# RmsNorm on one Trainium2 core: sums of squares accumulated in PSUM by eight 128x512 products, root and reciprocal on full tiles

## What is computed

```python
def rms_norm(x, g, eps=RMS_EPS):
    xf = x.astype(jnp.float32)
    y = xf * lax.rsqrt(jnp.mean(xf * xf, axis=-1, keepdims=True) + eps)
    return (y * g.astype(jnp.float32)).astype(x.dtype)
```

## Time and profile before

| | |
|---|---|
| three runs | 4704.64, 4706.24, 4707.51 us, median 4706.24 |
| span of the profiled execution, first to last instruction | 4705.5 us |
| mean granted clock of TensorE | 0.894 |
| TensorE, weight loads, VectorE, ScalarE busy | 86%, 68%, 44%, 29% of the span |
| line 501, 288 records | 60.1 us busy, 168.5 us idle before it, ended by line 520 |
| line 506, 144 records | 37.2 us busy, 21.2 us idle before it |
| line 520, 102 additions | 63.1 us busy |

### The profile page before, as it was taken

One profiled execution on the slowest core, in us unless ns is written; L12 is line 12 of the kernel. 1 busy time (PEld: TensorE's weight loads), 2 busy tenths in 40 slices (PEclk: granted clock), 3 DMA queues, 4 the chain that ended last, 5 costly groups with the idle time before them and its releaser, 6 DMA issues. The chain is left out here.

```text
span 4705.5 us, 54624 instructions
## 1 busy us (share of the span) xinstructions
PE 4033.5 (86%) x21065; PEld 3196.7 (68%) x21065; DVE 2084.3 (44%) x3286; ACT 1342.8 (29%) x1844; POOL 0.2 (0%) x4
## 2 busy tenths in 40 slices
PE   5899998988999798699978799782599957897998
PEld 4667886767788684588866688681477734676886
DVE  2374544134445424533243433426666644524333
ACT  2353433232343323232232332213211112223222
POOL 0000000000000000000000000000000000000000
PEclk9999998975899897799987899885699966998999
DMA  2201222210122220022210122210000000021221
GB/s 98 75 0 63 96 91 81 90 54 0 63 98 93 79 82 35 36 89 92 96 67 27 63 89 98 87 48 22 5 0 0 0 9 27 0 89 63 98 96 65
DMA packets 43350, 278.44 MB, mean 59 GB/s; under 512 B 5920, under 2 KB 6816, under 8 KB 10598
## 3 DMA queue, kind: packets, MB, share of 16 engines
q1 hardware_dynamic: 36576, 266.35, 16.0%
q10 hardware_dynamic: 6662, 10.53, 0.7%
HBM read 274.76 MB, written 2.11 MB: 59 GB/s over the span
## 5 line engine op out<-in xcount | busy, mean ns | idle before, releaser
L190 PE MATMUL PS<-XH,WH 128*128 128x512 f32 (+1 forms) x2848 | 1104.3, 388 | 75.0 <-DVEq L95 34.3
L191 PE MATMUL PS<-XL,WH 128*128 128x512 f32 (+1 forms) x2848 | 1106.4, 388 | 0.0
L192 PE MATMUL PS<-XH,WL 128*128 128x512 f32 (+1 forms) x2848 | 1100.2, 386 | 0.0
L146 DVE TENSOR_TENSOR WL<-W,WH 128x2048 fp32r<-128x2048 f32 x254 | 582.0, 2292 | 1007.2 <-ACT WH L136 1002.8
L136 ACT ACTIVATE WH<-W 128x2048 fp32r<-128x2048 f32 x254 | 485.4, 1912 | 1102.3 <-PE PS L260 686.5
L190 PEld LDWEIGHTS PS<-XH,WH 128*128 128x128 f32 x2848 | 540.7, 190 | 209.0 <-issue 61.2
L192 PEld LDWEIGHTS PS<-XH,WL 128*128 128x128 f32 x2848 | 541.8, 190 | 112.0
L191 PEld LDWEIGHTS PS<-XL,WH 128*128 128x128 f32 x2848 | 540.9, 190 | 111.7
L258 PE MATMUL PS<-HH,WH 128*128 128x512 f32 (+1 forms) x1024 | 402.0, 393 | 10.5 <-DVEq L95 9.3
L259 PE MATMUL PS<-HL,WH 128*128 128x512 f32 (+1 forms) x1024 | 400.3, 391 | 0.0
L260 PE MATMUL PS<-HH,WL 128*128 128x512 f32 (+1 forms) x1024 | 399.8, 390 | 0.0
(11 more groups left out here) (437 smaller groups left out, 5045.8 us busy)
## 6 DMA issues: line engine op xcount, KB each, us to landing
W<-in_weights SPq DMA_DIRECT2D x254, 1024.0 KB, 4.8
X<-in_x ACTq DMA_DIRECT2D x1, 2048.0 KB
out<-X ACTq DMA_DIRECT2D x1, 2048.0 KB, 7.1
consts<-in_consts ACTq DMA_DIRECT2D x1, 1025.0 KB
bias<-bias_spread ACTq DMA_DIRECT2D x4, 256.0 KB
w_gd<-in_w_gd ACTq DMA_DIRECT2D x1, 640.0 KB
rope<-in_c_rope ACTq DMA_DIRECT2D x1, 528.0 KB
ws<-in_ws ACTq DMA_DIRECT2D x1, 512.0 KB
```

Source lines behind the costliest of these rows:

```text
L146: P.e.tensor_tensor(K.WL[:, s, :], K.W[:, s, :], K.WH[:, s, :].bitcast(F32), ALU.subtract).then_inc(P.sem("weights_split"), P.adds("weight ...
L190: P.e.matmul(out, wh[:, k, c], xh[:, k, r], start=(k == 0), stop=False)
L191: P.e.matmul(out, wh[:, k, c], xl[:, k, r], start=False, stop=False)
L192: last = P.e.matmul(out, wl[:, k, c], xh[:, k, r], start=False, stop=(k == KT - 1))
```

## The change

`RmsNorm` no longer adds squares on VectorE and builds no diagonals. TensorE multiplies each of the eight tiles of squares, as moving operand, by the 128x128 matrix of 1/1024 and accumulates in one PSUM bank (two with 528 tokens), which gives the mean already spread over the partitions. ScalarE takes the root from PSUM with eps as bias, on 128x512, into `R`; VectorE takes the reciprocal of 128x512 in place, and scales the tiles by `R` in SBUF instead of a row in PSUM. A pair of columns with eps joins the constants. Two counts of `norm_mean` keep `CentreV`'s semaphore in step.

```diff
     def act(self, K, P):
...
         split_last(K, P, split_act)
-        P.e.wait_ge(P.sem("norm_inverse"), P.due("norm_inverse"))
-        for r in self.columns(K):
-            last = P.e.activation(r, r, ACT.Sqrt)
+        P.e.wait_ge(P.sem("norm_mean"), P.due("norm_mean"))
+        for part, (t0, tn) in enumerate(self.toks):
+            last = P.e.activation(K.R[:, t0:t0 + tn], K.PS[:, part, 0:tn], ACT.Sqrt, bias=K.eps_col[:, 0:1])
         last.then_inc(P.sem("norm_root"), P.adds("norm_root"))
...
     def pe(self, K, P):
 
-        P.e.wait_ge(P.sem("norm_summed"), P.due("norm_summed"))
-        for j, (part, c, n) in enumerate(self.blocks()):
-            t = self.toks[part][0] + c
-            for half in range(2):
-                last = P.e.matmul(K.PS[0:n, 0, 2 * j:2 * j + 2], K.Y[:, half, t:t + n], K.inv_d[:, 0:2], start=(half == 0), stop=(half == 1))
+        for k in range(KT):
+            P.e.wait_ge(P.sem("norm_squared"), P.due("norm_squared"))
+            for part, (t0, tn) in enumerate(self.toks):
+                last = P.e.matmul(K.PS[:, part, 0:tn], K.inv_d[:, :], K.Y[:, k, t0:t0 + tn], start=(k == 0), stop=(k == KT - 1))
         last.then_inc(P.sem("norm_mean"), P.adds("norm_mean"))
-
-        for j, (part, c, n) in enumerate(self.blocks()):
-            P.e.wait_ge(P.sem("norm_diagonal"), P.due("norm_diagonal"))
-            last = P.e.matmul(K.PS[:, 6 + part, c:c + n], K.ones_row[0:n, 0:128], K.R[0:n, 16 + 128 * (j % 4):16 + 128 * (j % 4) + n], start=True, stop=True)
-            last.then_inc(P.sem("norm_spread"), P.adds("norm_spread"))
...
     def dve(self, K, P):
 
-        for k in range(2, KT):
-            P.e.wait_ge(P.sem("norm_squared"), P.due("norm_squared", 3 if k == 2 else 1))
...
-            last = P.e.tensor_tensor(y, y, K.Y[:, k, self.t0:self.t1], ALU.add)
...
+        P.count("norm_mean", 1)
         split_last(K, P, split_dve)
...
+        P.e.wait_ge(P.sem("norm_root"), P.due("norm_root"))
+        P.e.reciprocal(K.R[:, self.t0:self.t1], K.R[:, self.t0:self.t1]).then_inc(P.sem("dve_order"), P.adds("dve_order"))
         P.e.wait_ge(P.sem("dve_order"), P.due("dve_order", 0))
...
-            P.e.tensor_scalar(K.R[0:n, at:at + n], K.ident[0:n, 0:n], K.R[0:n, j:j + 1], None, ALU.mult).then_inc(P.sem("norm_diagonal"), P.adds("norm_diagonal"))
...
+        r = K.R[:, self.t0:self.t1]
```

More of the change, by code:

```diff
@@ L468 @@
     after_sums = before_panels = False
-    def blocks(self):
-        out = [(part, c, min(128, tn - c)) for part, (t0, tn) in enumerate(self.toks) for c in range(0, tn, 128)]
-        return sorted(out, key=lambda b: -b[2])
-    def columns(self, K):
-        n, rows = len(self.blocks()), self.blocks()[-1][2]
-        return [K.R[:, 0:4]] + ([K.R[0:rows, 4:n]] if n > 4 else [])
     def act(self, K, P):
@@ L513, in dve @@
     def dve(self, K, P):
-        for k in range(2, KT):
-            P.e.wait_ge(P.sem("norm_squared"), P.due("norm_squared", 3 if k == 2 else 1))
-            if k >= 4:
-                P.e.wait_ge(P.sem("norm_partial"), P.due("norm_partial", 0, less=1))
-            y = K.Y[:, k % 2, self.t0:self.t1]
-            last = P.e.tensor_tensor(y, y, K.Y[:, k, self.t0:self.t1], ALU.add)
-            last.then_inc(P.sem("norm_summed" if k == KT - 1 else "norm_partial"), P.adds("norm_summed" if k == KT - 1 else "norm_partial"))
-        split_last(K, P, split_dve)
-        blocks = self.blocks()
-        P.e.wait_ge(P.sem("norm_mean"), P.due("norm_mean"))
-        for j, (part, c, n) in enumerate(blocks):
-            last = P.e.tensor_scalar(K.R[0:n, j:j + 1], K.PS[0:n, 0, 2 * j:2 * j + 1], self.eps, None, ALU.add)
-        last.then_inc(P.sem("dve_order"), P.adds("dve_order"))
-        P.e.wait_ge(P.sem("dve_order"), P.due("dve_order", 0))
-        for r in self.columns(K):
-            last = P.e.reciprocal(r, r)
-        last.then_inc(P.sem("norm_inverse"), P.adds("norm_inverse"))
-        P.e.wait_ge(P.sem("norm_root"), P.due("norm_root"))
-        for j, (part, c, n) in enumerate(blocks):
-            if j >= 4:
-                P.e.wait_ge(P.sem("norm_spread"), P.due("norm_spread"))
-            at = 16 + 128 * (j % 4)
-            P.e.tensor_scalar(K.R[0:n, at:at + n], K.ident[0:n, 0:n], K.R[0:n, j:j + 1], None, ALU.mult).then_inc(P.sem("norm_diagonal"), P.adds("norm_diagonal"))
-        P.e.wait_ge(P.sem("norm_spread"), P.due("norm_spread", min(4, len(blocks))))
-        two = len(self.toks) == 2
-        r = K.PS[:, 6:8, 0:self.toks[0][1]] if two else K.PS[:, 6, 0:self.toks[0][1]]
-        view = (lambda ap: ap.rearrange("p (a n) -> p a n", a=2)) if two else (lambda ap: ap)
+        P.count("norm_mean", 1)
+        split_last(K, P, split_dve)
+        P.e.wait_ge(P.sem("norm_root"), P.due("norm_root"))
+        P.e.reciprocal(K.R[:, self.t0:self.t1], K.R[:, self.t0:self.t1]).then_inc(P.sem("dve_order"), P.adds("dve_order"))
+        P.e.wait_ge(P.sem("dve_order"), P.due("dve_order", 0))
+        r = K.R[:, self.t0:self.t1]
+        view = lambda ap: ap
         lag = 2
@@ L2353 @@
 CONSTS = [("ident", 128), ("inv_d", 128), ("inv_dv", 128), ("causal", 128), ("ones_row", 512), ("reset64", 512),
-          ("causal64", 256), ("one_col", 2), ("flip", 128), ("keep_upper", 128)]
+          ("causal64", 256), ("one_col", 2), ("flip", 128), ("keep_upper", 128), ("eps_col", 2)]
 def program(nc, args, out):
@@ L2385, in program @@
         K.ones_row, K.reset64, K.causal64, K.one_col = cols["ones_row"], cols["reset64"], cols["causal64"], cols["one_col"]
-        K.flip, K.keep_upper = cols["flip"], cols["keep_upper"]
+        K.flip, K.keep_upper, K.eps_col = cols["flip"], cols["keep_upper"], cols["eps_col"]
         K.p, at = {}, 0
@@ L2622, in make_consts @@
         "flip": np.eye(128)[::-1],
+        "eps_col": np.full((128, 2), EPS),
         "keep_upper": (r[:, None] <= r[None, :]).astype(np.float32),
```

## The result

| | before | after |
|---|---|---|
| median of four runs each | 4705.44 us | 4726.31 us |
| lowest, highest | 4698.37, 4707.51 | 4722.60, 4728.48 |
| span of the profiled execution | 4705.5 us | 4725.9 us |
| mean granted clock | 0.894 | 0.903 |

The changed kernel takes 1.0044 times as long as the one before (95% interval 1.003 to 1.0059): 20.9 us slower. The forecast was 4725.3 us, +19.1. How far that was for the right reasons is the subject of what follows.

The account below looks back on a forecast made before the run. In each norm three engines work in turn, every hand-over on the path, bounding time to first scaling. Terms 4.5 - 0.5 + 6.5 + 6.4 + 2.2 = +19.1 us on the 4706.24 median gave 4725.3 us, range 4715 to 4738.

Parts of the forecast that it names:

- The chains: In each norm, from last sum, last addition or first square to first scaling; all seventeen together +19.1 us.
- attention stretch: From sixth norm's first scaling through wide stage, differential attention and narrow stage to seventh norm's squares; no change forecast.
- Nine norms behind a narrow stage: Norms after a narrow stage, without the final one: last sum to first scaling 11.4 for 10.9 us, +4.5.
- first rival: Clock falls in the short idle time before ten norms behind narrow stages: 2.7 us more each, +27, 4752 us; 6 in 100.
- Final norm: The last norm, where ScalarE starts its squares later: last sum to first scaling 11.4 for 11.94 us, -0.5.
- Prices of root, reciprocal and scaling: Steps after the products: root 0.68 us, reciprocal 3.35, hand-overs 0.10, scalings from SBUF no dearer; 4.1 us to first scaling.
- fourth rival: A step costs what no row shows, slower root or scalings; 0.05 us on 136 scalings gives +7, 4732 us; 10 in 100.
- Cold starts: Seven norms where TensorE has long been idle: eight products take 9.88 us with hand-over (10.19 with 528 tokens).
- three terms: Cold-start norms: three at the start or behind loads +6.5, two behind adding norms +6.4, two with 528 tokens +2.2 us.
- second rival: TensorE is at full clock in all norms: seven norms save 2.7 us each, -19, 4706 us; 4 in 100.
- things at zero: Eps constant, root's table load and first wide panel were taken to cost nothing; panels might save 0.5 us in seven places.
- third rival: Products of the ten norms start right behind the last narrow product, 0.8 us earlier each: -8, 4717 us; 5 in 100.

Follow-up runs that it names:

- second profile: The changed kernel run once more with nothing altered, for its profile: 4725.14 us, span 4723.3 us.
- shifted kernels: The kernel before with one added VectorE reciprocal in the sixth norm, of 128x256 or 128x128 constants: 4710.26 us and 4716.03 us.

## Why the prediction came out right, and where it did not

**The time was right, and partly by luck: two errors cancel.** The chains were forecast at +19.1 and are +14.9 (+15.4 in the second profile); the attention stretch was forecast at zero and is +5.4 in the profiled execution and +2.0 in the second one.

- **Nine norms behind a narrow stage: right.** Forecast 9 x (11.4 - 10.9) = +4.5, measured +4.80: 11.38 in each. Start 0.10 for 0.13, products 7.13 at full clock, then 4.15 for 4.13. The nine were not quite as alike before as the prediction says: three took 10.49, 10.77 and 10.82 us, which makes the 0.3. Taking the products from CentreV's warm row held in all ten, so the first rival (clock falls in the 0.83 us of idle) is out.
- **Final norm: right**, -0.4 for -0.5.
- **Prices of root, reciprocal and scaling: right.** 0.69 for 0.68, 3.35 for 3.35. The doubled reciprocal shows that it is on the path but for 0.14 us, and three scalings from SBUF take 2.08 as forecast, so the fourth rival falls too. On the reciprocal the Trainium skill ("VectorE: DVE Perf Modes", the fixed hardware budget) would have given 4.27 by my estimate; fifteen records with a mean of 3.353 stand against it.
- **Cold starts: the failed step.** "Since the clock rose in the row of the same work, the row itself is nearest": 9.88 us for seven norms. Measured, the products took 8.87, 9.89 and 9.45 at the start and behind loads, 8.57 and 8.55 behind adding norms, 9.14 and 9.49 with 528 tokens (for 10.19). How soon the clock rises after the first product varied from norm to norm, by the clock records from 2.9 us to 5.6, and was 5.5 in the row that the price came from the earlier trace rows; one row can't tell that it is at the long end. It mis-sized the three terms: +5.7 for +6.5, +3.9 for +6.4, +0.9 for +2.2, together 4.6 us too much. It is not the second rival: nowhere did such a norm start warm. In the second profile of the change it was 8.53 to 9.81, and each place had its own time again within 0.1 us, except the one at the start (9.61 for 8.87). So the time goes with the place more than with chance; why is open.
- **The unchanged stretches: wrong as a list of things at zero.** I wrote that I should be wrong "if a stage between norms changed its length by more than a us", and two did: the attention stretch, +5.38, and the rest behind the tenth norm, -1.11. The second profile of the change and the shifted kernels show that the former needs no cause in the changed stages. The latter was -1.18 in the second profile and was not looked into. The saving of up to 3.5 us in first panels did not come where a wide stage follows at once (rests behind the second, fourth, eighth, twelfth and sixteenth norm are within 0.06 us of before's).
- **The third rival** needed the wait away; with the wait in place it did not occur, as the listing of waits said. Taken away, the chains fell by 19 us.

In terms of sizes: of the 20.9 us that the medians show, about 15 are the change's own. The interval of the measured ratio, 14 to 28 us, holds both numbers. Since the stretch came out 3.4 us apart in two profiles of the very same kernel, the 5.4 can't be counted as its lasting cost; that the stretch is longer with the change on average isn't excluded, as it was so in both profiles, and the medians lie 6 us further apart than the chains explain. What remains open is why the clock falls and rises where it does in the attention: the runs show that it differs between executions of one kernel and between kernels, but not by what rule, nor whether a shift ahead of the stretch moves it. Nor was a norm tried with additions where TensorE starts cold and full products where it is warm, which the 13.3 and 14.9 us behind loads suggest.

## What to carry to other kernels

When an engine's work is moved off a short serial chain, price what takes its place on the same chain: here eight float32 products and a full-tile reciprocal cost slightly more than the additions, diagonals and spreading that they replaced (11.38 us for 10.9), and only single-pass products (2.12 us for 7.13) made the idea pay. Once the chain shrinks, ask stage by stage what hides the work that used to stand under it: the same late split was free before a projection and cost up to 6.9 us before a load. And before a difference of some 5 us is put down to an edit, compare stretch by stage with the granted clock beside it; a total alone would have called a change of 15 us one of 20.

## What the runs showed of the hardware

- **A stretch with many short stalls differs in length with the clock.** The same 323 TensorE records of the attention took 102.2 to 118.0 us, in step with the time spent at clock 0.50 (45.7 us at 102.2, 53.8 at 106.4, 65.8 at 111.8, 79.1 at 118.0). Two executions of the changed kernel had 111.8 and 108.3. The Trainium skill ("TensorE: Matmul & The Clock Gate", what's actually happening) has the clock follow activity; no run here shows what in the attention's activity decides between these lengths.
- **A cold start has no fixed price.** Eight float32 products of 128x512 took 8.53 to 10.13 us after an idle stretch (two profiles of the change and that of the doubled reciprocal), 7.13 without.
- **Single-pass products are over three times as fast; small ones are not cheap in proportion.** 2.12 us for eight of 512 columns against 7.13, both at full clock. Products of two columns took 0.12 each at full clock and 0.22 at the low one, so 32 of them cost more than eight full tiles.
- **Small loads wait beside a large one.** The loads behind the fifth norm took 3.35 us to the next square alone and 7.98 next to 1 MB of weights, whose own landing went from 4.6 to 7.5 us; with the weights out of the way again they took 3.46.
